# Work moved from VectorE to GpSimd in front of an expert loop

## The reference

```python
g_idx = argmax(h @ w_group + b_group)                  # 4 groups, one is taken
e_prob = softmax(logits of the 8 experts in that group)
top_p, top_i = top_k(e_prob, 2);  top_p /= sum(top_p)  # two experts of 32 per token
weights = g_prob[g_idx] * top_p
order = argsort(expert ids);  counts = bincount(...)   # token lists, expert by expert
for each block of tokens of one expert e:
    y = (silu(xb @ w_gate[e]) * (xb @ w_up[e])) @ w_down[e]
out = segment_sum(y * weight, token)
```

## Time and profile before

| | |
|---|---|
| runs of the kernel | 1150.19 us median of 3 (1149.35 to 1150.51) |
| profiled execution | 1148.85 us, span 1147.0 us |
| busy: TensorE, its weight loads | 1103.0 us (96%), 600.0 us (52%) |
| busy: VectorE, ScalarE, GpSimd | 672.4 us (59%), 372.9 us (33%), 67.5 us (6%) |
| TensorE's mean granted clock | 0.987 |
| chain that ended last | TensorE 85%, VectorE 7%, ScalarE 2% |
| DMA | 243.20 MB, mean 212 GB/s over the span |

### The profile page before, as it was taken

How to read it: one execution, slowest core, us unless ns; L and a number is a source line. 1 busy time by engine, 2 the same in 40 slices (tenths; PEclk the granted TensorE clock), 3 DMA queues, 4 the chain that set the end, 5 groups by cost and what they waited for, 6 DMA issues and landing times.

```text
span 1147.0 us, 16734 instructions
## 1 busy us (share of the span) xinstructions
PE 1103.0 (96%) x4876; PEld 600.0 (52%) x4876; DVE 672.4 (59%) x1580; ACT 372.9 (33%) x811; POOL 67.5 (6%) x123
## 2 busy tenths in 40 slices
PE   7999999999799999999999999999997999999997
PEld 4854555556574444444457545555566544444443
DVE  4236765467685555555652477655667755555554
ACT  5226331114433333333252263210243433333332
POOL 1000000000007000000000000000000250000001
PEclk9999999999889999999999999999997999999999
DMA  9031024500319999999641300245005299999992
GB/s 351 2 109 39 1 74 147 220 1 1 151 73 406 417 421 421 423 422 422 263 157 44 103 1 1 75 147 220 1 2 220 108 404 422 421 423 422 421 422 105
DMA packets 50925, 243.20 MB, mean 212 GB/s; under 512 B 6512, under 2 KB 16784, under 8 KB 25520
## 3 DMA queue, kind: packets, MB, share of 16 engines
q1 hardware_dynamic: 50048, 240.78, 52.6%
q0 software_dynamic: 384, 1.31, 0.3%
q10 hardware_dynamic: 432, 0.38, 0.1%
HBM read 240.36 MB, written 2.10 MB: 211 GB/s over the span
## 4 chain that ended last, share of the span: by engine, by line
PE 85%; DVE 7%; ACT 2%; issue 2%; DMA 1%; DVEq 1%; ACTq 0%; POOLq 0%; SPq 0%
PE ps L2756 19%; PE ps L2300 12%; PE ps L2782 10%; PE ps L2564 9%; PE ps L2290 7%; PE ps L2717 6%; PE ps L2718 5%; PE ps L2268 5%; PE ps L2612 2%; PE ps L2383 2%; PE ps L2327 2%; DMA X<-in_x 1%; PE ps L2422 1%; PE ps L2619 1%; DVE xlo L2013 1%
## 5 line engine op out<-in xcount | busy, mean ns | idle before, releaser
L2756 PE MATMUL ps<-wgu,xw 128*64 128x512 f32 x1024 | 225.2, 592 | 0.2
L2127 DVE TENSOR_TENSOR X<-ps,X 128x512 f32<-128x512 f32 x253 | 154.5, 682 | 6.9 <-issue 6.1
L2300 PE MATMUL ps<-hT,ring 128*128 128x512 f32 x352 | 156.8, 595 | 0.0
L2756 PEld LDWEIGHTS ps<-wgu,xw 128*64 128x64 f32 x1024 | 73.5, 137 | 145.7 <-issue 144.0
L2782 PE MATMUL ps<-wdn,hhT 128*64 128x512 f32 x512 | 116.9, 598 | 0.0
L974 ACT ACTIVATE xw<-xgT 128x512 f32 (+1 forms) x132 | 81.9, 624 | 107.3 <-issue 92.9
L2564 PE MATMUL ps<-ring,yT 128*128 128x512 f32 x256 | 115.0, 596 | 0.9 <-DVE ssqY L1798 0.8
L2717 PE MATMUL ps<-yhi,Wt 128*128 128x512 f32 x256 | 106.6, 416 | 0.2
L2300 PEld LDWEIGHTS ps<-hT,ring 128*128 128x128 f32 x352 | 64.6, 190 | 69.8 <-issue 69.8
L2718 PE MATMUL ps<-ylo,Wt 128*128 128x512 f32 x256 | 100.9, 394 | 0.0
L2148 DVE SCALAR_TENSOR_TENSOR ylo<-ps,ws,yhi 128x512 fp32r<-128x512 f32 x64 | 48.1, 751 | 63.8 <-ACTq L1370 63.3
(11 more groups left out here) (364 smaller groups left out, 1344.5 us busy)
## 6 DMA issues: line engine op xcount, KB each, us to landing
wgu<-in_w_gate SPq DMA_DIRECT2D x64, 1024.0 KB, 10.3
wgu<-in_w_up SPq DMA_DIRECT2D x64, 1024.0 KB, 12.4
wdn<-in_w_down SPq DMA_DIRECT2D x64, 1024.0 KB, 12.6
ring<-in_w_in SPq DMA_DIRECT2D x8, 1024.0 KB, 6.6
ring<-in_w_mix_out SPq DMA_DIRECT2D x12, 512.0 KB, 6.3
w_kv<-in_xa_w_kv SPq DMA_DIRECT2D x4, 1024.0 KB, 8.5
ring<-in_w_in SPq DMA_DIRECT2D x2, 2048.0 KB, 15.5
ring<-in_w_in SPq DMA_DIRECT2D x2, 1536.0 KB, 14.0
```

The source lines that it names most:

```text
L2127: tt(xh, bank, xh, ALU.add).then_inc(mfreed((what, n)), 1)
L2300: last = mm(bank, w[:, c, c0:c0 + P], hT[:, c, :], start=c == 0, stop=c == KD - 1)
L2756: last = mm(bank[r], xw[:, c, j, 0:SLOTS], wgu[2 * parity + j][:, :, c, :], start=c == 0, stop=c == KD - 1)
```

## The change

- `list_spans` goes from VectorE to GpSimd, which also makes the zero columns of xgT and the low parts of tiles 2 and 3, each in two operations (a multiply into `scaled_x`, which shares xlo's place, and a subtraction) in place of one. TensorE waits for `low_ready` for these tiles. VectorE waits for `spans_ready` ahead of `tiles_past`.
- On VectorE `one_hot(3)` follows `one_hot(2)`, `tiles_past` and `padded_places` come before the gains of half 1, and `ranks_shown` with `params_free` comes before the first pair's step instead of within it.
- `all_ones` and `diag` are of the rounded kind, so that the places product is.

```diff
@@ semaphores, tiles
-        all_ones = rt[:, 5]
+        all_ones = at("all_ones", [P, P], F32R, o + 8192 + 5 * 4 * NT * NE)
-        diag = at("diag", [P, 2 * NT, P], F32, late + 4096)
+        diag = at("diag", [P, 2 * NT, P], F32R, late + 4096)
+        scaled_x = at("scaled_x", [P, NT, D], F32, late)
@@ GpSimd
+            def list_spans():
+
+                n_lists = HALVES * NE
+                second_rank = rt[:, 0].rearrange("p (t e) -> p t e", t=NT)[:, NT // HALVES:NT]
+                combined(rt[:, 1, 2 * NE:3 * NE], row(1), rt[:, 1, NE:2 * NE], ALU.add)
+                combined(second_rank, second_rank, row(1).unsqueeze(1).to_broadcast([P, NT // HALVES, NE]), ALU.add)
+                scaled(rt[:, 4, n_lists:n_lists + NE], row(1), float(SLOTS), None, ALU.min)
+                pool.drain()
+                nc.gpsimd.tensor_copy(spans, rt[:, 4, 0:3 * NE])
...
+                def low_part(t):
+
+                    wait_apart(pool, S["xhi_ready"], done(l, "xhi_ready", t + 1))
+                    scaled(scaled_x[:, t], X[:, t], rstd_x[:, t:t + 1], None, ALU.mult)
+                    pool.drain()
+                    combined(xlo[:, t], scaled_x[:, t], xhi[:, t].bitcast(F32), ALU.subtract)
+                    pool.drain()
+                    pool.nop().then_inc(S["low_ready"], 1)
+
+                wait_apart(pool, S["rank_kept"], done(l, "rank_kept", 1))
+                list_spans()
+                pool.memset(xgT[:, :, 2 * SEQ:SORTED], 0.0)
+                pool.drain()
+                pool.nop().then_inc(S["spans_ready"], 1)
+                low_part(2)
+                low_part(3)
                 wait_apart(pool, S["params_free"], l + 2)
                 overflow_table()
@@ VectorE
-                def list_spans():
-
-                    dve.wait_ge(S["rank_kept"], done(l, "rank_kept", 1))
-                    ts(rt[:, 4, n_lists:n_lists + NE], first_count, float(SLOTS), None, ALU.min)
-                    tt(counts, first_count, rt[:, 1, NE:2 * NE], ALU.add)
-                    tt(rank[:, 2:4], rank[:, 2:4], first_count.unsqueeze(1).to_broadcast([P, 2, NE]), ALU.add)
-                    dve.drain()
-                    nc.vector.tensor_copy(spans, rt[:, 4, 0:3 * NE])
-                    signal("spans_ready")
...
-                    nc.vector.memset(all_ones, 1.0)
+                    ts(all_ones[:], iota[:, 0:P], 0.0, 1.0, ALU.mult, ALU.add)
...
                     else:
-                        ranks_shown()
-                        signal("params_free")
                         slot_weights()
...
                 ts(dest_2[:], dest[:], -float(SEQ), None, ALU.add)
-                list_spans()
+                dve.drain()
                 one_hot(2)
-                low_part(2)
-                nc.vector.memset(xgT[:, :, 2 * SEQ:SORTED], 0.0)
+                one_hot(3)
                 sorted_gain(0)
-                low_part(3)
-                one_hot(3)
+                dve.wait_ge(S["spans_ready"], done(l, "spans_ready", 1))
                 tiles_past()
+                dve.drain()
+                padded_places()
                 sorted_gain(1)
-                padded_places()
                 placed()
                 chosen(rank_k, rank)
                 token_weights()
+                ranks_shown()
+                signal("params_free")
                 step_(0, 0, False)
@@ TensorE
-                    wait_apart(pe, S["xlo_ready"], done(l, "xlo_ready", t + 1))
+                    if t < 2:
+                        wait_apart(pe, S["xlo_ready"], done(l, "xlo_ready", t + 1))
+                    else:
+                        wait_apart(pe, S["low_ready"], done(l, "low_ready", t - 1))
...
-                        mm(bank, all_ones, diag[:, NT * k:NT * (k + 1), :], start=True, stop=True
+                        mm(bank, all_ones[:], diag[:, NT * k:NT * (k + 1), :], start=True, stop=True
```

More of the change, by code:

```diff
@@ L400 @@
     max_ready=14, p_ready=14, pn_ready=14, x1_updated=NT, x2_updated=NT, G_ready=NT, G_used=2,
-    xgT_act=KD, xgT_dve=KD, xw_half=1, spans_ready=1, params_free=1, place_ready=1, ranked_ready=1, places_ready=2, ws_ready=1, rank_read=1, rank_kept=1,
+    xgT_act=KD, xgT_dve=KD, xw_half=1, spans_ready=1, low_ready=2, params_free=1, place_ready=1, ranked_ready=1, places_ready=2, ws_ready=1, rank_read=1, rank_kept=1,
     qx_ready=NT, qx_squared=NT, xq_ssq=NT, qx_reduced=NT, qxT_ready=NT, oTx_ready=NT, lg_ready=NT,
-    xhi_ready=NT, xlo_ready=NT, x_final=NT, M_ready=1, exp_arg=1, exp_done=1, route_ready=1, layer_done=1,
+    xhi_ready=NT, xlo_ready=2, x_final=NT, M_ready=1, exp_arg=1, exp_done=1, route_ready=1, layer_done=1,
 )
@@ L2006, in _ @@
                 signal("rank_read")
-                rank, first_count, counts = r32(0), row(1), rt[:, 1, 2 * NE:3 * NE]
+                rank, counts = r32(0), rt[:, 1, 2 * NE:3 * NE]
                 chosen(dest, r32(5), slice(0, NT // HALVES))
```

## The result

The changed kernel takes 1156.26 us (median of 6 runs, 1155.08 to 1157.94), beside 1149.39 for the kernel before (6 runs, 1149.16 to 1150.51): a ratio of 1.0059, with a 95% interval of 1.0046 to 1.0072. It is slower by 6.9 us. The forecast was 1150.6 with a range up to 1155.5, so the time lies above both. (The forecast added 0.4 us to 1150.19, the median of three runs that was known then; over six runs the kernel before stands at 1149.39, so its base was 0.8 too high and the gap is the wider for it.) The profiled execution has a span of 1153.4, against 1147.0: 6.4 more.

A forecast was written before the change was run, and what follows sets the result against it. TensorE was taken to bound the loop, VectorE's chain its start; per layer -2.0 + 2.2 = +0.2, twice +0.4 on the profiled 1148.85 gave 1149.25, with the median 1.34 above it 1150.6, range 1146.0 to 1155.5.

The forecast's parts named there:

- What bounds it: Expert loop: TensorE is busy throughout, so a change in front is worth what it moves the loop's start.
- Part 1: VectorE's shortened list in front of gate-up: without contention, gate-up starts 1.04 us earlier in each layer.
- Part 2: Behind gate-up: rounded places product and earlier ranks start the slot-weight product 8.55 instead of 9.53 us behind; 0.95 gained.
- Part 3: Cost to VectorE, in front of gate-up, of GpSimd's low-part work on shared ports: +2.2 us per layer.
- one hold: Tile 2's subtraction on GpSimd makes one VectorE operation, in one_hot(2), stand: 2.2 us per layer; chance 0.44.
- the row at 349.88: Earlier trace: a VectorE operation not late beside GpSimd's one-input operation from 349.26, read as one-input operations not holding VectorE.
- The rival that took the hold as long as the instruction: GpSimd's multiplies also hold VectorE, throughout, in front of gate-up: +7.2 us per layer, 1164.6; chance 0.10.
- the rival of two holds: Tile 3's subtraction also holds VectorE, before one_hot(3)'s second operation: 2.2 us per layer more, 1155.0; chance 0.20.
- Its sign, a one_hot(3) of over 3 us: On VectorE's timeline, a one_hot(3) longer than 3 us would show that two subtractions hold VectorE.

The follow-up runs named there:

- the kernel without low parts: The changed kernel with GpSimd's four operations for the low parts of tiles 2 and 3 left out: 1143.88 us, ratio 0.9955 to the kernel before.
- multiply on ScalarE: The changed kernel with the low parts' multiplies on ScalarE and GpSimd's subtractions held back until the fourth one-hot is made: 1148.33 us, ratio 0.9985 to the kernel before.
- rounded kind only: The kernel before with only the places product in the rounded kind: 1152.71 us, ratio 1.0034 to the kernel before.
- the cut kernel: As "multiply on ScalarE", with tile 3's subtraction cut in two of 512 elements: 1145.27 us, ratio 0.9972 to the kernel before.
- before + multiplies: The kernel before with only the two 1024-element multiplies added on GpSimd, results unread: 1152.16 us, ratio 1.0029 to the kernel before.
- before + both: The kernel before with both multiplies and both subtractions of 1024 elements added on GpSimd, results unread: 1160.94 us, ratio 1.0106 to the kernel before.
- subtractions later: The changed kernel with both multiplies first and GpSimd's subtractions held back until the fourth one-hot is made: 1152.55 us, ratio 1.0029 to the kernel before.

## Why the forecast was wrong, step by step

**What bounds it:** held. A change in front of the loop moved the loop by its whole amount: the stretches' sum above closes on 6.4 us with 0.7 over.

**Part 1, VectorE's list free of holds:** held. Forecast −1.04 in front of gate-up, measured −1.25 (20.89 against 22.14) in the kernel without low parts.

**Part 2, behind gate-up:** held. Slot-weight product 8.47 behind gate-up (forecast 8.55), the transposes at 8.15 (forecast 8.15), ranks over at 6.33 (forecast 6.3). To the down product it is −1.16, where I had −0.95. The experiments add what I hadn't seen: it takes the rounded product, the early ranks and the moved padded places together, and the product alone costs 3.8 us by TensorE's clock.

**Part 3, GpSimd's low parts:** this is the step that failed. I took one hold, of 2.0 to 2.2 us in each layer, and put +2.2 into the sum; the term measured 5.61 and 6.00. There were five, of 5.60 us, in layer 0, and four, of 5.25 us, in layer 1, where TensorE at its lower clock added 0.75. Three things of it were off:

- "That a one-input GpSimd operation holds too, the row at 349.88 speaks against." It does hold, for its first 0.9 us, and one-input operations of VectorE again near its end. The row that I read the earlier trace rows begins 0.62 behind the start of a 512-element operation, half as long; if the held parts are half as long too, which no run shows, it falls between them. From this came 0.65 + 0.73 at starts and 0.29 at an end, 1.67 us in layer 0. The rival that took the hold as long as the instruction was wrong on the other side: it put 2.5 and 2.7 on the two multiplies.
- The small operations were over at 316.34, not at 318.0: they hardly waited. So the multiply began 1.7 earlier than I placed it, and the subtraction at 320.03 fell on the places of the second half (1.99), as in the rival of two holds.
- VectorE, late by these, reached one_hot(3)'s second operation at 326.77, 0.2 behind the second subtraction's start; 1.94 more. I had that subtraction at 327.2 beside gains, and its place was nearly right (326.57). What moved was VectorE: each hold keeps it longer within reach of the next GpSimd operation. The rival of two holds named this meeting but asked for a multiply under 2.6 us; it took 3.24 and 2.85, and the meeting came all the same. Its sign, a one_hot(3) of over 3 us, is there (325.91 to 329.46), and its 1155.0 lies near the result, but by luck in part: its two long holds are 3.93 of the 5.60 us, and the rest are the multiply's, which it took as none.

The prices of the operations were right: 2.85 and 2.34 alone, against 2.82 and 2.35. (They add up to 5.17, not the 5.3 of the text, and the rival in which the multiply holds throughout to +7.3, not +7.2; neither changes the forecast.) The forecast's own sum with the measured sizes, on the profiled execution: 1148.85 − 2 × 2.0 + 5.61 + 6.00 for the low parts = 1156.46; parts 1 and 2 gave 0.42 a layer more, 1155.6; the stretch between the layers, the tail and the later first comparison −0.4, 1155.2. The changed kernel's profiled execution took 1155.24, and its median stands 1.0 above that.

**TensorE's clock** stood in no step. It explains 0.75 us of the result (layer 1, included in the 6.00). In the experiments a fall behind gate-up costs 1.7 us ("multiply on ScalarE") to 3.3 us ("rounded kind only").

What stays open: when an idle stretch brings the clock down. In "rounded kind only", TensorE was busy 4.19 of 340 to 345 in layer 0 and kept 1.00, and 3.73 of 906 to 911 in layer 1 and fell; in the cut kernel it fell behind a smaller gap (0.41 idle from 344 to 346), where the kernel without low parts kept 1.00 with the same gap (0.40 idle from 341 to 346). Nor does any run say why the stretch between the layers was 0.66 shorter in after.

## What to carry to other kernels

Before work goes from VectorE to GpSimd, lay the two timelines side by side and count every VectorE operation on SBUF that would meet a large GpSimd one; a two-input operation of 1024 elements costs VectorE more (2.0 us) than the low part cost it to make (1.29). What must go to GpSimd belongs beside VectorE's work from PSUM and, where it laps over that, in smaller pieces; a step that an idle ScalarE can do costs nothing. A shorter product is no gain while its successor waits for something else, and the idle time that it leaves TensorE can cost more than the product did.

## What the runs showed of the hardware that I had not expected

- GpSimd's multiply by a per-partition scalar (one input, 1024 elements, 2.86 us) holds VectorE's operations on SBUF until 0.90 to 0.98 behind its start: in "before + multiplies" at 315.71 and 318.86, in "before + both" at 314.32 and 320.47, in the change at 316.64, 323.56 and, in layer 1, 891.78 (a multiply that waited for VectorE and took longer for it, 3.18 or 3.24, is counted from 2.86 before its end).
- Later in the same multiply VectorE's operations with two SBUF inputs run freely (325.04 at 0.75 in the change), those with one don't: the change's 325.91 and, in "subtractions later", 324.81 were let go 0.21 before the multiply's end, having begun 2.35 and 1.97 behind its start. One that lay from 1.22 to 1.71 behind it (layer 1 of the change, 893.00) took its 0.49. That the multiply reads first and writes last would explain this; no run tests it.
- Four multiplies of 256 cost GpSimd up to 5.07 us beside a busy VectorE where one piece of 1024 takes 2.86.
- Idle times of TensorE of 0.4 to 3.9 us were in some places followed by a few us at the 1.2 GHz level (3.88 in the change), in others not (0.40 without low parts); gate-up to slot-weight product then took 1.7 us more, the slot-weight product itself up to 1.36.
